# Processing the experts of a mixture layer in an order made on the chip from their numbers of blocks

## The chip, the cores and the metric

The kernel runs on one core of a Trainium2 chip. The metric is the device time of one execution in microseconds (us). Three runs of the kernel before took 956.48, 958.35 and 960.37 us, median 958.35. The profiled execution took 958.9 us; its span, from the first to the last instruction of the core, is 956.8 us.

## The reference

One encoder layer over 768 tokens of width 1024 (256 of a prompt, 512 of a sample): an input projection, neighbourhood attention, a convolution module, an output projection, and then a mixture of 32 experts. Only the mixture matters here:

```
g_sel = argmax(h @ w_group + b_group)                  # one group of 4
top_v, top_j = top_k(h @ w_expert[g_sel] + b_expert, 2)  # two of its 8 experts
counts = bincount(expert_idx, length=32)
hid = silu(x_b @ w_gate[e]) * (x_b @ w_up[e])
y   = hid @ w_down[e]                                  # per block of rows of one expert
```

Gate and up weights are 1024 x 512, the down weight is 512 x 1024, all float32, so an expert has three matrices of 2 MB. The order in which experts are worked through does not enter the result. The two results of a token are weighted by its gates and added to it, and a final RMS norm follows.

## The kernel before

The routing is made on the chip. Each token picks two experts, and the rows of an expert are packed into blocks of 64 (BLK). An expert has as many blocks as its rows need, and at least one. With the reference's inputs the counts of rows give 39 blocks: experts 5, 7, 21, 24 and 31 have two, expert 28 has three, and the other 26 have one. Blocks are numbered from 0 to 38 in the order of the experts 0 to 31.

VectorE (DVE) computes the routing in one chain (lines 1750 to 1801): from the logits to one-hot choices, a running count `before`, two matmuls on TensorE (PE) that give each token's rank within its expert (lines 1172 and 1173), the number of blocks of each expert (`nblk`), their running sum (`endb`, `startb`), from that the row that each token gets, and an index list `idx` (line 1801). DVE also writes `table`, integers in SBUF from which the engines read loop bounds: 32 numbers of blocks, 32 first blocks, 32 last blocks and two counts.

Weights lie in three slots. The experts at positions 0, 3, 6, ... use slot 0, those at 1, 4, 7, ... slot 1 (both in `ring`), those at 2, 5, 8, ... slot 2 (in `big`). Experts 0, 1 and 2 are loaded before the routing is known (lines 741 to 768). From then on SyncE (SP) runs `load_expert` (line 729) for positions 3 to 31: six transfers of 1 MB each, two halves of gate and up (the first pair when PE has passed the first half of the gate and up work of the last block that uses the slot, the second pair when it has passed the second), and two halves of down when the block's down work is done. All go through SP's one queue, in this order.

PE runs `expert` (line 1246) for the 32 positions: for each block, gate and up matmuls (lines 1201 and 1204), which wait for the four halves one by one, then transposes of the hidden rows and of the next block's rows (lines 1216 and 1192), then down matmuls (lines 1238 and 1239), which wait for the two down halves. ScalarE (ACT) applies Silu, DVE multiplies, and ACT and DVE take the result out of PSUM with the gates (line 1840 is DVE's part, the last work of a block but for the store). GpSimd (POOL) gathers the 64 rows of a block from DRAM four blocks ahead (line 885, 256 KB), and stores the results by an indirect transfer into `results` (line 900, 256 KB).

The last two blocks (37 and 38) are not stored. When the store of block 36 has landed, SP issues twelve reads of 512 KB of `results` into slot 2 (lines 778 to 782). POOL adds them in pairs (line 955), DVE adds the first four pairs to `x` (line 1851) right after the last block's result, PE adds the last two blocks by one-hot matmuls (line 1268; for tiles 4 and 5 also the pairs, line 1271), DVE takes each tile's sum (line 1890), ACT squares, POOL takes the root (line 830), DVE scales (line 1895) and SP stores the output (line 785).

## Time and profile before

| | us |
|---|---|
| median of three runs | 958.35 (956.48 to 960.37) |
| profiled execution | 958.9 |
| its span | 956.8 |
| PE busy | 851.9 (89% of the span) |
| DVE busy | 425.4 (44%) |
| ACT busy | 248.9 (26%) |
| POOL busy | 156.7 (16%) |

The page gives busy times of the engines over the whole span, then the span in 40 equal slices of 23.92 us with the DMA engines' busy share and what they moved, then the chain of work that ended last and the costliest groups of instructions. The expert stage begins at about 399 us and its last block ends at 925 us; what lies before is the same in both kernels but for a few constants. "Busy" of DMA is the mean over the core's 16 DMA engines.

### The profile page before, as it was taken

Reading aid. Unit: us, or ns where it says so; the run is one execution under the profiler, and the core shown is the slowest. Engines: PE = TensorE matmul, PEld = TensorE weight load, DVE = VectorE, ACT = ScalarE, POOL = GpSimd, SP = SyncE. Lnnn points to the kernel's source line nnn. Section 1 sums busy time; section 2 is a strip of 40 time slices with the busy share of each in tenths; the row PEclk is TensorE's granted clock in tenths of the full one; section 3 lists DMA queues with packets and bytes.
Section 4 is the critical chain, followed back from the end, with each engine's and each line's share of the span. In section 5 each row is a group of like instructions: output and inputs, shape, how many; then the busy total and the mean of one; then the engine's idle time right before and its main releaser. Section 6 shows DMA issues by size and latency. Waiting matters only on the chain.

```text
span 956.8 us, 15627 instructions
## 1 busy us (share of the span) xinstructions
PE 851.9 (89%) x5808; PEld 579.0 (61%) x5809; DVE 425.4 (44%) x622; ACT 248.9 (26%) x486; POOL 156.7 (16%) x286
## 2 busy tenths in 40 slices
PE   3989999999869995599999998888789989889985
PEld 2879978778558884455555554444445556455542
DVE  5399979857987433522222221212121222122265
ACT  5214273664655222011111111111011111111112
POOL 4100010000001000212222222111112222121162
PEclk9989999999979996599999999999999999999997
DMA  7443435221084637699999999999999999999464
GB/s 200 121 123 107 157 143 187 68 77 45 4 245 192 253 143 292 243 356 405 390 399 398 397 405 400 413 403 416 401 412 412 392 393 387 399 402 396 160 242 132
DMA packets 80891, 265.75 MB, mean 278 GB/s; under 512 B 18093, under 2 KB 43949, under 8 KB 56281
## 3 DMA queue, kind: packets, MB, share of 16 engines
q1 hardware_dynamic: 63232, 245.10, 67.2%
q0 software_dynamic: 7808, 18.54, 5.6%
q10 hardware_dynamic: 9816, 1.66, 0.9%
q8 instruction: 21, 0.34, 0.1%
q14 instruction: 14, 0.11, 0.0%
HBM read 247.52 MB, written 27.08 MB: 287 GB/s over the span
## 4 chain that ended last, share of the span: by engine, by line
PE 64%; DMA 17%; SPq 8%; DVE 6%; issue 2%; ACT 1%; ACTq 0%; POOL 0%; POOLq 0%; DVEq 0%
PE ps L1201 15%; PE ps L999 12%; DMA ring<-in_w_up 10%; PE ps L1238 9%; SPq L723 7%; PE ps L1121 7%; PE ps L995 4%; DMA ring<-in_w_down 3%; DMA big<-in_w_up 3%; PE ps L1204 3%; PE ps L1192 2%; DVE big L1585 2%; PE ps L1216 2%; PE ps L1018 1%; PE ps L1048 1%
## 5 line engine op out<-in xcount | busy, mean ns | idle before, releaser
L1204 PE MATMUL ps<-ring,big 128*64 128x256 f32 x896 | 208.5, 391 | 23.6 <-DMA ring<-in_w_up 23.5
L1201 PE MATMUL ps<-ring,big 128*64 128x256 f32 x896 | 210.2, 391 | 3.7 <-DMA ring<-in_w_gate 2.5
L1201 PEld LDWEIGHTS ps<-ring,big 128*64 128x64 f32 x896 | 124.3, 141 | 60.8 <-issue 15.4
L1204 PEld LDWEIGHTS ps<-ring,big 128*64 128x64 f32 x896 | 124.8, 141 | 54.0 <-DMA ring<-in_w_up 32.2
L1831 DVE TENSOR_TENSOR big<-ps,big 64x256 f32<-64x256 f32 x78 | 33.2, 426 | 263.9 <-ACT big L1482 263.9
L999 PE MATMUL ps<-hT,w_split 128*128 128x512 f32 (+1 forms) x768 | 145.2, 344 | 4.1 <-DVE hT L1541 3.6
L999 PEld LDWEIGHTS ps<-hT,w_split 128*128 128x128 f32 x768 | 118.0, 190 | 25.6 <-issue 11.3
L1585 DVE SCALAR_TENSOR_TENSOR big<-big,vec 128x783 f32<-128x783 f32 x116 | 119.6, 1031 | 3.0
L1482 ACT ACTIVATE big<-ps 64x256 f32<-64x256 f32 x78 | 29.3, 375 | 285.9 <-PE ps L1204 285.9
L1238 PE MATMUL ps<-ring,big 128*64 128x512 f32 x224 | 102.3, 599 | 0.3 <-DMA ring<-in_w_down 0.3
L1239 PE MATMUL ps<-ring,big 128*64 128x512 f32 x224 | 102.4, 599 | 0.0
L1204 PE MATMUL ps<-big 128*64 128x256 f32 x352 | 80.2, 386 | 7.1 <-DMA big<-in_w_up 7.1
L1840 DVE TENSOR_SCALAR big<-ps,gate_of 64x512 f32<-64x512 f32 x39 | 29.5, 756 | 122.5 <-PE ps L1239 122.5
L1201 PE MATMUL ps<-big 128*64 128x256 f32 x352 | 80.7, 385 | 0.5 <-DMA big<-in_w_gate 0.5
L897 POOL COPY to_of<-idx 64x1 uint32 x37 | 18.7, 506 | 331.4 <-DVE big L1840 331.4
L1121 PE MATMUL ps<-wo_split,hT 128*128 128x512 f32 x288 | 70.2, 402 | 2.1 <-issue 2.1
L1121 PEld LDWEIGHTS ps<-wo_split,hT 128*128 128x128 f32 x288 | 55.0, 194 | 13.4 <-issue 2.1
L1201 PEld LDWEIGHTS ps<-big 128*64 128x64 f32 x352 | 48.4, 139 | 23.6 <-issue 5.2
L1494 ACT ACTIVATE big<-ps,gate_of 64x512 f32<-64x512 f32 x39 | 26.6, 681 | 131.7 <-PE ps L1239 131.7
L1238 PEld LDWEIGHTS ps<-ring,big 128*64 128x64 f32 x224 | 28.1, 136 | 50.5 <-issue 48.7
L1204 PEld LDWEIGHTS ps<-big 128*64 128x64 f32 x352 | 48.4, 139 | 16.8 <-DMA big<-in_w_up 9.9
L1192 PE MATMUL ps<-ident,spare 64*128 64x64 f32 x320 | 41.9, 272 | 1.2 <-DVE spare L1856 1.2
(213 smaller groups left out, 1119.4 us busy)
## 6 DMA issues: line engine op xcount, KB each, us to landing
ring<-in_w_gate SPq DMA_DIRECT2D x44, 1024.0 KB, 28.0
ring<-in_w_up SPq DMA_DIRECT2D x44, 1024.0 KB, 28.8
ring<-in_w_down SPq DMA_DIRECT2D x44, 1024.0 KB, 29.4
big<-in_w_gate SPq DMA_DIRECT2D x20, 1024.0 KB, 29.0
big<-in_w_up SPq DMA_DIRECT2D x20, 1024.0 KB, 29.6
big<-in_w_down SPq DMA_DIRECT2D x20, 1024.0 KB, 29.2
w_raw<-in_w_in SPq DMA_DIRECT2D x20, 512.0 KB, 4.0
results<-spare POOLq DMA_DIRECT2D x12, 512.0 KB, 2.9
```

The lines of the kernel that those rows point to most:

```text
L723: sp.dma_start(to[:, ks, :], src).then_inc(landed, 16)
L995: mm = pe.matmul(ps[:, n % 2, 0:2 * P], hT[:, k // 4, hi_h, k % 4, g * P:(g + 1) * P], split_of(2 * c)[:, :, hi_w, k, :], **flags)
L999: mm = pe.matmul(ps[:, n % 2, 0:size], w_split[:, sub, hi_w, k, :], hT[:, k // 4, hi_h, k % 4, cols], **flags)
L1121: mm = pe.matmul(ps[:, OUT_BANK[g], :], mT[:, part, hi_m, k, t * P:(t + 1) * P], wo_split[n % 2][:, hi_w, k, :], start=(k == 0 and m == 0) ...
L1192: mm = pe.transpose(ps[:, 4, k * BLK:(k + 1) * BLK], xb[:, k:D:KD], ident[0:BLK, 0:BLK])
L1201: pe.matmul(ps[0:BLK, 6 * h, 0:FH], xT[:, k, :], gate_w[s][:, k, fs], start=(k == 0), stop=(k == KD - 1))
L1204: mm = pe.matmul(ps[BLK:2 * BLK, 6 * h + 1, 0:FH], xT[:, k, :], up_w[s][:, k, fs], start=(k == 0), stop=(k == KD - 1))
L1238: pe.matmul(ps[0:BLK, 2, :], hbT[:, k, :], down_w[s][:, k, 0:512], start=(k == 0), stop=(k == KF - 1))
L1239: mm = pe.matmul(ps[BLK:2 * BLK, 3, :], hbT[:, k, :], down_w[s][:, k, 512:1024], start=(k == 0), stop=(k == KF - 1))
L1585: link(nc.vector.scalar_tensor_tensor(conv[:, j % 2, :], z, w, conv[:, j % 2, :], ALU.mult, ALU.add))
L1831: nc.vector.tensor_tensor(hb[:, fs], ps[BLK:2 * BLK, 6 * h + 1, 0:FH], sG[:, fs], ALU.mult).then_inc(hb_ready[h], 1)
L1840: nc.vector.tensor_scalar(yb2[q][:, 512:1024], ps[BLK:2 * BLK, 3, :], gate_of[q][BLK:2 * BLK], None, ALU.mult).then_inc(evacuated, 1)
```

## The change

Experts 0, 1 and 2 stay first. The other 29 are ranked by their number of blocks, more first, the lower number first among equals, and a fixed pattern `PLACES` says which rank goes to which position (place): ranks 20 to 23 to places 3 to 6, ranks 24 to 28 (the fewest blocks) to places 27 to 31, ranks 6 down to 0 (the most blocks) to places 8, 11, 14, ..., 26, and the rest to the places between. Blocks are numbered by places. The order is made in the routing chain: DVE writes a key, compares all pairs of keys, PE sums the comparisons over partitions, DVE finds the place of each expert, PE and DVE turn the numbers of blocks into running sums by place and back to the experts' numbers, and `table` gets 32 entries more, the expert at each place. SP reads the expert from the table before it loads a place.

With the counts of the reference's inputs the places get the experts 0, 1, 2, 19, 20, 22, 23, 18, 3, 11, 17, 31, 10, 16, 24, 9, 15, 21, 8, 14, 7, 6, 13, 5, 4, 12, 28, 25, 26, 27, 29, 30. The numbers of blocks by place are 1 at places 0 to 10, then 2 1 1 2 1 1 2 1 1 2 1 1 2 1 1 3 at places 11 to 26, and 1 at places 27 to 31. By places before they are 1 1 1 1 1 2 1 2, then 1 at places 8 to 20, then 2 1 1 2 1 1 1 3 1 1 2.

```diff
+PLACES = [((0, 3, 1), E - 3, 1), ((8, 27, 3), 6, -1), ((9, 25, 3), 12, -1), ((7, 26, 3), 19, -1), ((3, 7, 1), 20, 1), ((27, 32, 1), 24, 1)]
+AT_ONCE = 3
 NB = MAXB + 2
...
@@ -727,9 +738,9 @@
                     load(e, *l)
             def load_expert(i, s):
-                e = SLOTS * i + s
-                end = sp.value_load(table[0:1, bass.ds(e + (2 * E - SLOTS), 1)], min_val=1, max_val=MAXB)
+                place = SLOTS * i + s
+                e = sp.value_load(table[0:1, bass.ds(place + (3 * E + 2), 1)], min_val=0, max_val=E - 1)
+                end = sp.value_load(table[0:1, bass.ds(place + (2 * E - SLOTS), 1)], min_val=1, max_val=MAXB)
                 sp.wait_ge(gu_half, end)
                 load_some(e, s, 0, 2)
...
             nc.gpsimd.memset(onesr[:], 1.0).then_inc(consts, 1)
+            link(nc.gpsimd.iota(key_first, [[-1, E]], base=0, channel_multiplier=0, allow_small_or_imprecise_dtypes=True))
+            nc.gpsimd.iota(key_first[:, 0:AT_ONCE], [[-BLK * MAXB, AT_ONCE]], base=-BLK * MAXB, channel_multiplier=0,
+                           allow_small_or_imprecise_dtypes=True).then_inc(consts, 1)
+            for (first, end, step), rank, by in PLACES:
+                nc.gpsimd.iota(rank_at[:, first:end:step], [[by, len(range(first, end, step))]], base=rank, channel_multiplier=0,
+                               allow_small_or_imprecise_dtypes=True).then_inc(consts, 1)
+            nc.gpsimd.memset(ends[:, 0:1], 0.0).then_inc(consts, 1)
             def root(out, in_, scale, ready, n):
...
@@ -1167,10 +1186,21 @@
-            pe.wait_ge(both_ready, 1)
+            pe.wait_ge(order_ready, 1)
             n = SLOTS8 * E - 1
             pe.matmul(ps[:, 0, 0:n], ones[:], before[:, 0:n], start=True, stop=False)
-            pe.matmul(ps[:, 0, 0:n], tri[:], both[:, 1:n + 1], start=False, stop=True).then_inc(rank_done, 1)
+            pe.matmul(ps[:, 0, 0:n], tri[:], both[:, 1:n + 1], start=False, stop=True).then_inc(order_ps, 1)
+            pe.wait_ge(x2_done, len(OUT))
+            pe.wait_ge(order_ready, 2)
+            pe.matmul(ps[0:E, 1, 0:1], behind, ones[0:E, 0:1], start=True, stop=True).then_inc(order_ps, 1)
+            pe.wait_ge(order_ready, 3)
+            pe.matmul(ps[:, 3, 0:E], column[:, 1:2].to_broadcast([E, P]), from_place, start=True, stop=True).then_inc(order_ps, 1)
+            pe.wait_ge(order_ready, 4)
+            pe.matmul(ps[:, 1, E:2 * E], column[:, 2:3].to_broadcast([E, P]), ident[0:E, 0:E], start=True, stop=True).then_inc(order_ps, 1)
+            pe.matmul(ps[:, 3, E:2 * E], token[0:E, 0:1].to_broadcast([E, P]), at_place, start=True, stop=True).then_inc(order_ps, 1)
             for a in range(2 * NT):
...
@@ -1759,17 +1789,36 @@
                 link(V.tensor_tensor(sel[:, j].rearrange("p t (g e) -> p t g e", g=G), within_groups(j), in_group, ALU.mult))
             dve.wait_ge(zero_out, 16 * ZERO_TILES)
             link(V.tensor_tensor(both.rearrange("p (e t) -> p t e", t=SLOTS8)[:, 1:NT + 1, :], sel[:, 0], sel[:, 1], ALU.add))
-            V.tensor_tensor_scan(before, again[:], both, 0.0, ALU.mult, ALU.add).then_inc(both_ready, 1)
+            V.tensor_tensor_scan(before, again[:], both, 0.0, ALU.mult, ALU.add).then_inc(order_ready, 1)
             V.tensor_tensor(dd[:], m2[:], m1[:], ALU.subtract).then_inc(dd_ready, 1)
-            dve.wait_ge(rank_done, 1)
+            dve.wait_ge(order_ps, 1)
             rank = ps[:, 0, 0:SLOTS8 * E].rearrange("p (e t) -> p e t", t=SLOTS8)
+            rank_sb = rank_in.rearrange("p (e t) -> p e t", t=SLOTS8)
+            own = ident[0:E, 0:E]
+            def own_column(n, row):
+                return V.tensor_tensor_reduce(out=row_of, in0=row, in1=own if n < 2 else at_place, scale=1.0, scalar=0.0,
+                                              op0=ALU.mult, op1=ALU.add, accum_out=column[:, n:n + 1])
             link(V.tensor_tensor(cmpb, rank[:, :, NT:NT + 1].to_broadcast([P, E, MAXN]),
                                  thr[:].unsqueeze(1).to_broadcast([P, E, MAXN]), ALU.is_gt))
             link(V.tensor_reduce(nblk[:], cmpb, AX.X, ALU.add))
-            link(V.tensor_tensor_scan(endb[:], onesr[:], nblk[:], 0.0, ALU.mult, ALU.add))
-            link(V.tensor_tensor(startb[:], endb[:], nblk[:], ALU.subtract))
-            link(V.scalar_tensor_tensor(pos, startb[:].unsqueeze(2).to_broadcast([P, E, NT]), float(BLK), rank[:, :, 0:NT],
+            link(V.scalar_tensor_tensor(key, nblk[:], float(BLK), key_first, ALU.mult, ALU.add))
+            link(own_column(0, key[0:E]))
+            V.tensor_scalar(behind, key[0:E], column[:, 0:1], None, ALU.is_lt).then_inc(order_ready, 1)
+            link(own_column(1, nblk[0:E]))
+            dve.wait_ge(order_ps, 2)
+            link(V.tensor_scalar(at_place, rank_at[0:E], ps[0:E, 1, 0:1], None, ALU.is_equal))
+            V.tensor_tensor_scan(from_place, onesr[0:E], at_place, 0.0, ALU.mult, ALU.add).then_inc(order_ready, 1)
+            link(V.tensor_copy(rank_in, ps[:, 0, 0:SLOTS8 * E]))
+            dve.wait_ge(order_ps, 3)
+            link(V.tensor_copy(ends[:, 1:], ps[:, 3, 0:E]))
+            own_column(2, ends[0:E, 0:E]).then_inc(order_ready, 1)
+            dve.wait_ge(order_ps, 4)
+            startb = ps[:, 1, E:2 * E]
+            link(V.scalar_tensor_tensor(pos, startb.unsqueeze(2).to_broadcast([P, E, NT]), float(BLK), rank_sb[:, :, 0:NT],
                                         ALU.mult, ALU.add))
             link(V.tensor_tensor(posd, sel, pos.rearrange("p e t -> p t e").unsqueeze(1).to_broadcast([P, 2, NT, E]), ALU.mult))
             link(V.tensor_reduce(destf[:], posd, AX.X, ALU.add))
@@ -1786,15 +1835,18 @@
                                      block_at[:, j].unsqueeze(2).to_broadcast([P, NT, NB]), ALU.is_equal))
                 V.tensor_tensor(block_hot[:, some], block_hot[:, some], token[:, some].unsqueeze(2).to_broadcast([P, NT, NB]),
                                 ALU.mult).then_inc(onehot_ready, 1)
-            link(V.tensor_copy(table[0:1, 0:E], nblk[0:1, :]))
-            link(V.tensor_copy(table[0:1, E:2 * E], startb[0:1, :]))
-            link(V.tensor_scalar(even[:], even[:], endb[0:1, E - 1:E], None, ALU.is_lt))
+            link(V.tensor_tensor(table[0:1, 0:E], ends[0:1, 1:], ends[0:1, 0:E], ALU.subtract))
+            link(V.tensor_copy(table[0:1, E:2 * E], ends[0:1, 0:E]))
+            dve.wait_ge(order_ps, 5)
+            link(V.tensor_scalar(table[0:1, 3 * E + 2:], ps[0:1, 3, E:2 * E], -1.0, None, ALU.add))
+            link(V.tensor_scalar(even[:], even[:], ends[0:1, E:], None, ALU.is_lt))
             link(V.tensor_reduce(cnt2[:, 0:1], even[:], AX.X, ALU.add))
-            link(V.scalar_tensor_tensor(cnt2[:, 1:2], cnt2[:, 0:1], -2.0, endb[0:1, E - 1:E], ALU.mult, ALU.add))
+            link(V.scalar_tensor_tensor(cnt2[:, 1:2], cnt2[:, 0:1], -2.0, ends[0:1, E:], ALU.mult, ALU.add))
             link(V.tensor_scalar(cnt2[:, 1:2], cnt2[:, 1:2], -5.0, None, ALU.add))
-            link(V.tensor_copy(table[0:1, 3 * E:], cnt2[:]))
-            V.tensor_copy(table[0:1, 2 * E:3 * E], endb[0:1, :]).then_inc(table_ready, 1)
+            link(V.tensor_copy(table[0:1, 3 * E:3 * E + 2], cnt2[:]))
+            V.tensor_copy(table[0:1, 2 * E:3 * E], ends[0:1, 1:]).then_inc(table_ready, 1)
             dve.wait_ge(idx_ps, 1)
             link(V.tensor_scalar(nobody[:], ps[0:BLK, 5, 0:NB], 0.0, float(4 * T), ALU.is_equal, ALU.mult))
```

## Rows read from the trace of the kernel before

**Rows 1.** The page, part 2: what DMA moved in 40 slices of the span.
```profile
GB/s 200 121 123 107 157 143 187 68 77 45 4 245 192 253 143 292 243 356 405 390 399 398 397 405 400 413 403 416 401 412 412 392 393 387 399 402 396 160 242 132
```

**Rows 2.** Busy time by stretch of the expert stage; the columns are named above.
```profile
core 0: us, PE busy (x) PEld busy (x) DVE busy (x) ACT busy (x) POOL busy (x), PEclk, DMA share, GB/s
399.00:545.00 146.00, 144.89 (x1100) 86.36 (x1101) 35.74 (x60) 23.14 (x59) 31.80 (x58) 0.97 0.96 374
...
580.00:732.00 152.00, 126.44 (x859) 68.78 (x859) 28.07 (x48) 18.57 (x49) 24.32 (x45) 0.97 1.02 407
732.00:865.00 133.00, 124.48 (x922) 74.20 (x920) 29.78 (x50) 19.77 (x50) 27.01 (x50) 0.99 1.02 395
865.00:901.00 36.00, 36.00 (x280) 21.31 (x278) 8.96 (x15) 5.95 (x15) 6.71 (x12) 1.00 0.80 312
...
```

**Rows 3.** DVE in order of time: the last work of blocks 20, 32, 36, 37, 38.
```profile
682.76 0.76 DVE L1840 TENSOR_SCALAR big<-ps,gate_of 64x512 f32<-64x512 f32 x1 [3.25 <-PE ps L1239]
...
853.26 0.75 DVE L1840 TENSOR_SCALAR big<-ps,gate_of 64x512 f32<-64x512 f32 x1 [3.80 <-PE ps L1239]
...
901.26 0.76 DVE L1840 TENSOR_SCALAR big<-ps,gate_of 64x512 f32<-64x512 f32 x1 [3.26 <-PE ps L1239]
...
913.25 0.76 DVE L1840 TENSOR_SCALAR big<-ps,gate_of 64x512 f32<-64x512 f32 x1 [3.26 <-PE ps L1239]
925.24 0.76 DVE L1840 TENSOR_SCALAR big<-ps,gate_of 64x512 f32<-64x512 f32 x1 [0.57 <-PE ps L1239]
```

**Rows 4.** Chain of waits in order of time: three weight loads (start of issue, us).
```profile
645.90 27.90 DMA ring<-in_w_up
...
739.85 34.61 DMA ring<-in_w_up
...
821.20 29.85 DMA ring<-in_w_down
```

**Rows 5.** SP's queue in order of time: the first issues for places 7 and 8.
```profile
455.84 0.34 SPq L723 DMA_DIRECT2D ring<-in_w_gate  x1
...
479.82 0.34 SPq L723 DMA_DIRECT2D big<-in_w_gate  x1
```

**Rows 6.** DMA from 880 to 920 us, in slices of 1 us.
```profile
GB/s 401 426 426 438 311 287 266 365 316 254 254 229 188 266 188 180 102 115 102 70 25 16 0 0 0 111 0 131 385 430 377 410 414 422 418 422 406 418 414 418
```

**Rows 7.** The routing and the first block, in order of time, several engines.
```profile
384.37 0.22 DVE L1770 TENSOR_TENSOR_SCAN endb<-onesr,nblk 128x32 f32<-128x32 f32 x1
384.62 0.19 DVE L1771 TENSOR_TENSOR startb<-endb,nblk 128x32 f32<-128x32 f32 x1
384.85 0.35 DVE L1772 SCALAR_TENSOR_TENSOR big<-startb,ps 128x192 f32<-128x192 f32 x1
...
397.92 0.71 DVE L1856 COPY spare<-big 64x1024 f32<-64x1024 f32 x1 [3.22 <-DMA big<-h_rows,idx_of]
...
398.77 1.11 PE L1192 MATMUL ps<-ident,spare 64*128 64x64 f32 x8 [1.20 <-DVE spare L1856]
399.92 0.69 DVE L1820 COPY big<-ps 128x512 f32<-128x512 f32 x1 [1.29 <-PE ps L1192]
```

**Rows 8.** POOL in order of time, the first operation after its constants.
```profile
7.31 0.19 POOL L830 TENSOR_SCALAR r<-ss 128x1 f32<-128x1 f32 x1 [3.62 <-ACT big L1297]
```

**Rows 9.** The tail: SP's issues, DVE and PE, in order of time.
```profile
906.20 5.82 SPq L782 DMA_DIRECT2D big<-results  x12
...
926.02 5.33 DVE L1851 TENSOR_TENSOR x<-x,big 128x1024 f32<-128x1024 f32 x4
931.39 2.35 DVE L1890 TENSOR_TENSOR x<-x,ps 128x1024 f32<-128x1024 f32 x2
...
932.66 6.25 PE L1268 MATMUL ps<-big 128*128 128x512 f32 x10 [2.85 <-DVE x L1890]
```

**Rows 10.** POOL's pair sums (line 955) and the landing of the reads (line 782).
```profile
L955 POOL TENSOR_TENSOR big<-big x6: 2354/2360/2865, 911.3 to 924.0; 128x1024 f32<-128x1024 f32 x6
...
DMA to landing us min/median/max: 3.7/8.1/12.3
```

More of the change, by code:

```diff
@@ L524, in encoder @@
         nblk = sb("nblk", [P, E])
-        onesr = sb("onesr", [P, E]); endb = sb("endb", [P, E]); startb = sb("startb", [P, E])
+        ends = sb("ends", [P, E + 1])
+        onesr = sb("onesr", [P, E]); column = sb("column", [E, 4]); rank_in = after(SLOTS8 * E)
+        key, behind, at_place, from_place, row_of = (
+            junk[0:n, 2 * NT * NB + k * E:2 * NT * NB + (k + 1) * E] for k, n in enumerate((P, E, E, E, E)))
         again = sb("again", [P, SLOTS8 * E]); silu_first = sb("silu_first", [P, 1])
@@ L545, in encoder @@
         row_gates = sb("row_gates", [P, NB])
+        key_first, rank_at = row_gates[:, 0:E], row_tokens[:, 0:E]
         gate_of = [sb(f"gate_of{q}", [P, 1]) for q in range(2)]
         even = sb("even", [1, MAXPAIRS]); cnt2 = sb("cnt2", [1, 2])
-        table = sb("table", [1, 3 * E + 2], I32)
+        table = sb("table", [1, 4 * E + 2], I32)
         ps = ctx.enter_context(nc.psum_tensor("ps", [P, 8, 512], F32))
@@ L772, in _ @@
                     load_expert(i, s)
-            for e in range(E // SLOTS * SLOTS, E):
-                load_expert(e // SLOTS, e % SLOTS)
+            for place in range(E // SLOTS * SLOTS, E):
+                load_expert(place // SLOTS, place % SLOTS)
             pairs = sp.value_load(table[0:1, 3 * E:3 * E + 1], min_val=(E - 7) // 2, max_val=MAXPAIRS)
@@ L963, in _ @@
         def _(pe):
-            pe.wait_ge(consts, 14)
+            pe.wait_ge(consts, CONSTS)
             def turn_h(t):
@@ L1245, in _, with expert @@
             turn_rows()
-            def expert(e, s, target):
-                n = pe.value_load(table[0:1, bass.ds(e, 1)], min_val=1, max_val=MAXN)
-                first = pe.value_load(table[0:1, bass.ds(e + E, 1)], min_val=0, max_val=MAXB - 1)
+            def expert(place, s, target):
+                n = pe.value_load(table[0:1, bass.ds(place, 1)], min_val=1, max_val=MAXN)
+                first = pe.value_load(table[0:1, bass.ds(place + E, 1)], min_val=0, max_val=MAXB - 1)
                 with pe.Fori(0, n) as j:
@@ L1254, in _ @@
                     expert(SLOTS * i + s, s, 16 * i + 16)
-            for e in range(E // SLOTS * SLOTS, E):
-                expert(e, e % SLOTS, 16 * (e // SLOTS + 1))
+            for place in range(E // SLOTS * SLOTS, E):
+                expert(place, place % SLOTS, 16 * (place // SLOTS + 1))
             pe.wait_ge(late_ready, 1)
```

11 lines of the change are left out of this document (6 added, 5 removed).

## The prediction

> **What bounds the kernel now.** I read the page's slices first, then the stretches of the expert stage, then the ends of single blocks, the landings in the chain of waits, SP's queue, and last the routing chain and the tail. The slices show DMA at 385 to 416 GB/s from about 430 to 885 us [rows 1]. That is the stream of weights: 29 experts after the first three, 6 MB each. The stretches show two regimes [rows 2]. From 399 to 545 us PE is busy all the time (144.9 of 146 us), since three experts were loaded ahead. From 580 on PE waits (126.4 busy of 152 us), and DMA's share is 1.02: the stream is the bound there. From 865 to 901 PE is full again and DMA is not, because the stream runs out before the work does.
>
> A block that waits for nothing takes 12.0 us (913.25 to 925.24) [rows 3]. The stream's pace is 16.8 us per place: the last up half of place 18 landed at 645.90 + 27.90 = 673.80 and that of place 24 at 739.85 + 34.61 = 774.46, 16.8 each for six places [rows 4]. The last down half of place 28 landed at 821.20 + 29.85 = 851.05 [rows 4] and the last weights of all at about 901.5, where the slices of 1 us fall to nothing [rows 6], again 16.8 each for three places. So experts of one block starve PE, those of two (24 us) feed it, and the seven surplus blocks are worth something only while the stream still runs.
>
> The end is the point. Expert 28 has three blocks (the first ended at 853.26 [rows 3]) and expert 31 two, so when the last weights landed PE had just ended block 36 (901.26) and still had 37 and 38 to do, till 925.24 [rows 3]. That is 24 us of PE work behind the end of the stream, and then the tail: 956.8 - 925.2 = 31.6 us.
>
> **The change part by part.**
>
> *Length of the stream.* 29 places of 6 MB before and after, one after another. The first load waits for block 0 as before. In the front the new order has one block per place up to place 10; SP issues the load of place p+3 when the last block of place p has passed its first half, so single blocks let it issue earlier: before, the double of expert 5 held the issue for place 8 back to 479.82, 24 us after that for place 7 [rows 5]. DMA's share from 399 to 545 us is 0.96, so some 6 of 146 us were idle, the start included [rows 2], and I take 1 to 2 us as gained. Against it, one more block's rows will have been stored by the end of the stream (256 KB, 0.7 us at 400 GB/s). After the triple the load of place 29 is issued some 15 us before the queue is empty: block three of place 26 passes its first half about 28 us after block one began, while the last weights of place 26 land about 9 us after that beginning and those of the places 27 and 28 take 33.6 us more, 43 in all. So no gap. I leave the end of the stream at 901.5, between 898 and 905.
>
> *Work behind the stream.* Place 31 now has one block. A block that waits for its weights ends (start of line 1840) 9.0 us after the last up half (673.80 to 682.76) and at least 2.2 us after the last down half (851.05 to 853.26) [rows 3, 4]. The two down halves take 2 x 16.8 / 6 = 5.6 us after the last up, so the end comes 9.0 - 5.6 = 3.4 us after the last landing: 904.9. The other bound is PE's own: the last up half of place 26, the triple, lands at 774.46 + 2 x 16.8 = 808.1, its first block ends at 817.1, and seven more blocks of 12.0 follow: 901.1. The later counts, 904.9; with the pace a little slower in the middle both would meet near 905. Does PE reach place 26 in time? A group "2 1 1" takes 48 us of PE and 50.3 of the stream, so it arrives a little early each time. Before the routing's cost this is 925.2 - 904.9 = 20.3 us earlier.
>
> *The routing chain.* It is on the path: nothing of the expert stage starts before it. Removed are the sum and the difference at lines 1770 and 1771, 384.37 to 384.85, 0.48 us [rows 7]. Added on DVE ahead of the rows' places: key, own column, comparison, place, running sum, copy, own column, seven operations on 32 columns or less, at 0.19 to 0.22 us from those two rows and 0.03 between, 1.6 us. The copy of the ranks (256 columns, near the 0.35 us of line 1772 [rows 7]) and the second own column lie in the shadow of PE. Added are three round trips from DVE to PE and back. The nearest row is the one of eight transposes: DVE ends at 398.63, PE takes 398.77 to 399.88, DVE starts at 399.92, 1.3 us [rows 7]. With one small matmul instead of eight I take 0.8 each, between the bare handoffs of that row (0.14 and 0.04, say 0.2) and 1.3: 2.4 us, bounds 0.6 to 3.9; it is nearer to the upper row, whose work is of the same kind. One more operation stands ahead of the index list, 0.2. The sum is 1.6 + 2.4 + 0.2 - 0.5 = 3.7, taken as 4, with bounds of 2 and 5.5. All of the expert stage shifts by it, its stream too. The nine new constants of POOL at the start are hidden by the 3.6 us that POOL then waits for the first square sum [rows 8]; that holds while each takes under 0.4 us, and if one took more only the excess would count. SP's extra table read per place costs nothing while its queue is ahead by 28 us [rows 4]. Last work of block 38: 904.9 + 4 = 908.9, the stream's end 905.5.
>
> *The tail.* Before, SP issued the twelve reads of `results` at 906.20, 19 us before the last block ended [rows 9], on idle DMA; they landed 3.7 to 12.3 us after issue [rows 10], all ahead of use. A store lands 5 us after its block's end (901.26 to 906.20) [rows 3, 9]. Now the store of block 36 (place 29, two places of 16.8 us before 908.9) lands at about 880, and the reads stand in SP's queue behind the last weights. Loads land in the order of their issue at a steady pace [rows 4], so I let the reads land behind 905.5, 1.28 us each at the 410 GB/s of the reads in [rows 6]. Pair 0 is there at 908.1, and POOL adds a pair in 2.36 us [rows 10], so pair 3 is done at 918.0 and DVE's fourth addition (1.33 us by 5.33 / 4 [rows 9]) at 919.3. Before, the first sum with the last blocks (line 1890) started at 931.39 [rows 9]; all behind it stays as it is, the PE stretch of 6.25 us included. 931.4 - 919.3 = 12.1 us earlier: of the 16.3 us by which the last block ends earlier, 4.2 go to the wait for the reads. If the reads came earlier nothing is lost: bounds 0 and 7.
>
> The rule that bears on it stands in the Trainium skill, "DMA: Bandwidth & Descriptors", section "Queues, rings and completion order": each DMA engine takes the descriptors of one ring in order, and goes round between rings of different queues. By it the reads do wait behind the weights, and the stores on POOL's queue don't; no row of before has a read behind a weight load. Without the rule the time would be that of rival 1.
>
> Sum: span 956.8 - 12.1 = 944.7. The profiled execution lies 2.1 us above its span (958.9), so 946.8, and 0.55 above the median of 958.35: **946** us.
>
> **The rivals.** (1) The reads are not late: the sixteen engines of DMA don't finish together (the last weights trickle in from 885 to 901 [rows 6]), and the reads could fill that. Then the tail keeps its length: 942 us. (2) The stream starves somewhere, most likely after the triple, where the margin is smallest: if PE comes late to place 26 by one single block, the load of place 29 is issued late, and up to 7 us of stream are lost: 953. (3) The order doesn't do what it says (ranks or ties come out otherwise, or a place has another number of blocks): then only the 4 us of routing remain, 962. (4) Slower than before: the clock. PE now waits for weights from place 7 on, 90 us earlier than before. From block 7 (401 us, when the rows of block 0 are ready [rows 7], 3 more for its start at the low clock, and 7 x 12.0: 488) to 909 there are 421 us for 32 blocks, 13.2 us for each, so the plan holds down to a mean clock of 12.0 / 13.2 = 0.91 of full speed, and from 0.88 on all of the gain is gone. At 0.85 a block takes 14.1 us, 32 of them 452, and the time is 977. Against it: in the stretch where PE waits most today the clock is 0.97 [rows 2], with the same kind of waits, 4.8 us per single place.
>
> By the Trainium skill, "TensorE: Matmul & The Clock Gate", section "HAM oscillation — how this bites in real kernels", a stream of matmuls that waits for DMA at every tile can fall to the low clock at every tile; that would make rival 4 the forecast, with 977. The trace disagrees so far, by the 0.97.
>
> **How the numbers follow.** The forecast has 0.70, rival 1 0.12, rival 2 0.09, rival 3 0.05, rival 4 0.04. The range takes in the end of the stream (-3.5, +3.5), the routing (-2, +1.5) and the reads (-4.2, +2.8), whose full sums are 946 - 9.7 and 946 + 7.8; cut a little below, where three ends would have to meet, and with rivals 1 and 2 inside: 937 to 955. A measurement of this kernel tells some 0.5% from no change, which is below 953.6. Faster: 0.70 + 0.12 + two thirds of 0.09 = 0.88. Same: 0.03 + 0.05 = 0.08. Slower: 0.04.
>
> **What would show it.** The last weights land about as far after the routing as before, and only one block ends behind them, 3 to 4 us later. PE operations of lines 1201's kind on `big` (slot 2) go from 11 blocks to 17. PE starts to wait near place 7, about 490 us, and waits in small pieces to the end; its clock stays above 0.95. The first gate and up matmuls start about 4 us later. POOL's pair sums wait for reads, and DVE's four additions wait for POOL. I am wrong if the stream has a gap of more than 5 us, if the clock falls below 0.9, or if the routing takes over 7 us more.

## The result and the profile after

The changed kernel took 952.12 us in the median of four runs (950.59 to 953.14), the kernel before 958.95 on the same occasion (956.48 to 960.37). The ratio is 0.993, 95% interval 0.9905 to 0.9955: faster by 0.7%, or 6.8 us. The forecast was 946 (937 to 955), about 12 us faster. The sign, the range and the main mechanism held, but little more than half of the forecast gain came. The profiled execution has a span of 950.2 us against 956.8.

The end of the stages shows where it went. Below are two views of the changed kernel: what DMA moved by slice (the page, part 2), and busy time by stretch, columns as in [rows 2].

```profile
GB/s 202 120 120 117 155 143 188 68 79 45 1 222 221 211 188 240 280 263 405 403 390 399 404 415 399 396 399 393 402 401 396 401 404 390 406 383 405 394 208 133
```

```profile
core 0: us, PE busy (x) PEld busy (x) DVE busy (x) ACT busy (x) POOL busy (x), PEclk, DMA share, GB/s
403.00:545.00 142.00, 132.74 (x988) 78.45 (x990) 31.56 (x53) 20.27 (x51) 29.39 (x55) 0.97 0.96 377
545.00:580.00 35.00, 32.52 (x220) 17.95 (x218) 7.21 (x13) 4.91 (x13) 5.42 (x10) 0.95 1.01 402
580.00:732.00 152.00, 145.22 (x1102) 87.01 (x1098) 35.84 (x60) 23.87 (x60) 32.55 (x60) 1.00 1.02 399
732.00:865.00 133.00, 127.71 (x970) 75.41 (x968) 31.31 (x52) 20.57 (x51) 27.39 (x51) 1.00 1.01 398
865.00:906.00 41.00, 40.76 (x316) 24.42 (x312) 10.29 (x20) 7.00 (x18) 5.85 (x12) 1.00 0.99 395
906.00:924.00 18.00, 7.28 (x25) 2.45 (x24) 12.55 (x6) 0.96 (x2) 15.32 (x6) 0.79 0.49 199
```

The stream fills one slice more than before [rows 1], and DMA is at 0.99 up to 906 us, where before it had fallen to 0.80 in the last 36 us of the stream [rows 2]. PE's waits moved to the front (132.7 busy of 142 us), and in the stretch where it waited most before it is now nearly full (145.2 of 152, against 126.4), since the surplus blocks lie there. The clock is 0.95 or more in every stretch up to 906 us, so rival 4 is out.

DVE's last work of the blocks 37 and 38, to be compared with [rows 3]:

```profile
896.90 0.76 DVE L1892 TENSOR_SCALAR big<-ps,gate_of 64x512 f32<-64x512 f32 x1 [3.26 <-PE ps L1269]
909.76 0.76 DVE L1892 TENSOR_SCALAR big<-ps,gate_of 64x512 f32<-64x512 f32 x1 [2.79 <-PE ps L1269]
```

Block 38 reaches this point at 909.76, where 908.9 was forecast and 925.24 was the time before: 15.5 us earlier. But the span ends only 6.6 us earlier. The tail from this point to the end of the span was 956.8 - 925.2 = 31.6 us and is 950.2 - 909.8 = 40.4. It grew by 8.9 us, and 4.2 were forecast. Here is the tail in order of time, DVE and then POOL and SP; [rows 9] and [rows 10] answer to it.

```profile
910.93 1.22 DVE L1903 TENSOR_TENSOR x<-x,big 128x1024 f32<-128x1024 f32 x1 [0.41 <-POOL big L974]
914.39 9.91 DVE L1903 TENSOR_TENSOR x<-x,big 128x1024 f32<-128x1024 f32 x3 [2.23 <-POOL big L974]
924.33 2.35 DVE L1942 TENSOR_TENSOR x<-x,ps 128x1024 f32<-128x1024 f32 x2
...
908.55 17.96 POOL L974 TENSOR_TENSOR big<-big 128x1024 f32<-128x1024 f32 x6 [13.81 <-DMA big<-results]
...
893.99 13.35 SPq L793 DMA_DIRECT2D big<-results  x12
```

SP issued the reads at 893.99, and POOL could add the first pair at 908.55, as forecast (908.1). From there on it is slower than forecast. DVE's additions 2 to 4 take 9.91 us together, 3.3 each, where they took 5.33 / 4 = 1.33 before, and POOL's six pair sums fill 17.96 us without a gap, 3.0 each. DVE's fourth addition ends at 924.3, not at 919.3.

The groups of the two lines show the same by minimum, median and maximum in ns:

```profile
L974 POOL TENSOR_TENSOR big<-big x6: 2330/3316/3337, 908.5 to 923.2; 128x1024 f32<-128x1024 f32 x6
...
L1903 DVE TENSOR_TENSOR x<-x,big x4: 1224/3352/3356, 910.9 to 920.9; 128x1024 f32<-128x1024 f32 x4
...
L1942 DVE TENSOR_TENSOR x<-x,ps x6: 1211/1220/1221, 924.3 to 938.4; 128x1024 f32<-128x1024 f32 x6
```

Beside a pair sum of POOL, an addition of DVE that reads two tiles of SBUF takes 3.35 us instead of 1.22, and POOL's takes 3.32 instead of 2.33. The sums of line 1942, of the same size but with one operand in PSUM, take 1.22 throughout, the first of them beside POOL's last pair sum.

### The profile page after: what moved, and what is told of

It reads as the page before. It is cut to its first block, busy times and chain, and to the rows that moved or that the text cites. A ratio compares the mean times of both kernels' runs of the same rounds, so it can differ in the third digit from the quotient of the medians.

```text
span 950.2 us, 15799 instructions
## 1 busy us (share of the span) xinstructions
PE 845.7 (89%) x5816; PEld 579.1 (61%) x5817; DVE 428.7 (45%) x633; ACT 249.2 (26%) x486; POOL 161.5 (17%) x295
## 4 chain that ended last, share of the span: by engine, by line
PE 56%; DMA 23%; SPq 8%; DVE 7%; issue 2%; ACT 1%; POOL 1%; ACTq 0%; POOLq 0%; DVEq 0%
DMA big<-in_w_up 17%; PE ps L1018 12%; PE ps L1231 10%; PE ps L1140 7%; SPq L734 7%; PE ps L1268 7%; PE ps L1014 4%; DMA ring<-in_w_down 3%; PE ps L1234 2%; DVE big L1615 2%; PE ps L1222 2%; DMA big<-results 2%; PE ps L1037 1%; PE ps L1067 1%; PE ps L1246 1%
## 5 line engine op out<-in xcount | busy, mean ns | idle before, releaser
L1234 PE MATMUL ps<-ring,big 128*64 128x256 f32 x704 | 159.3, 384 | 6.7 <-DMA ring<-in_w_up 6.7
L1231 PE MATMUL ps<-ring,big 128*64 128x256 f32 x704 | 159.6, 384 | 1.7 <-DVE big L1872 1.1
L1018 PE MATMUL ps<-hT,w_split 128*128 128x512 f32 (+1 forms) x768 | 145.2, 344 | 4.0 <-DVE hT L1571 3.5
L1234 PE MATMUL ps<-big 128*64 128x256 f32 x544 | 123.7, 384 | 15.1 <-DMA big<-in_w_up 15.1
L1018 PEld LDWEIGHTS ps<-hT,w_split 128*128 128x128 f32 x768 | 117.9, 190 | 25.5 <-issue 11.2
L1231 PEld LDWEIGHTS ps<-ring,big 128*64 128x64 f32 x704 | 97.1, 139 | 58.0 <-issue 14.9
L1231 PE MATMUL ps<-big 128*64 128x256 f32 x544 | 124.4, 384 | 0.5 <-DMA big<-in_w_gate 0.5
L1234 PEld LDWEIGHTS ps<-ring,big 128*64 128x64 f32 x704 | 97.3, 139 | 14.0 <-DMA ring<-in_w_up 8.9
L1234 PEld LDWEIGHTS ps<-big 128*64 128x64 f32 x544 | 74.1, 138 | 33.7 <-DMA big<-in_w_up 20.5
L1231 PEld LDWEIGHTS ps<-big 128*64 128x64 f32 x544 | 74.2, 138 | 30.5 <-issue 8.1
L1268 PE MATMUL ps<-ring,big 128*64 128x512 f32 x176 | 80.4, 599 | 0.2 <-DMA ring<-in_w_down 0.2
L1269 PE MATMUL ps<-ring,big 128*64 128x512 f32 x176 | 80.4, 599 | 0.0
L1269 PE MATMUL ps<-big 128*64 128x512 f32 x136 | 62.4, 600 | 0.0
L1268 PE MATMUL ps<-big 128*64 128x512 f32 x136 | 62.3, 599 | 0.0
```

The source lines that it names most:

```text
L1018: mm = pe.matmul(ps[:, n % 2, 0:size], w_split[:, sub, hi_w, k, :], hT[:, k // 4, hi_h, k % 4, cols], **flags)
L1231: pe.matmul(ps[0:BLK, 6 * h, 0:FH], xT[:, k, :], gate_w[s][:, k, fs], start=(k == 0), stop=(k == KD - 1))
L1234: mm = pe.matmul(ps[BLK:2 * BLK, 6 * h + 1, 0:FH], xT[:, k, :], up_w[s][:, k, fs], start=(k == 0), stop=(k == KD - 1))
L1268: pe.matmul(ps[0:BLK, 2, :], hbT[:, k, :], down_w[s][:, k, 0:512], start=(k == 0), stop=(k == KF - 1))
L1269: mm = pe.matmul(ps[BLK:2 * BLK, 3, :], hbT[:, k, :], down_w[s][:, k, 512:1024], start=(k == 0), stop=(k == KF - 1))
```

## The experiments

The theory after the result: (a) the order puts the end of PE's work some 20 us earlier, less 4 us for the routing, by way of the stream of weights and what stands behind it; (b) the tail grew because the reads land late and because POOL's and DVE's sums, which lay under PE's last blocks before, now run at the same time and hinder each other. The rivals were that only the end of the order matters, that something else in the change made or cost the time, and for the tail that the late reads alone are the cause, or none of both. All kernels but one are edits of the changed kernel; times are medians beside runs of the kernel before on the same chip (958.2 to 958.6).

**The chain without the order.** Keys and places give back the experts' numbers.

```diff
-PLACES = [((0, 3, 1), E - 3, 1), ...]
+PLACES = [((0, 32, 1), 0, 1)]
...
-            link(nc.gpsimd.iota(key_first, [[-1, E]], base=0, ...))
+            link(nc.gpsimd.iota(key_first, [[-BLK * MAXB, E]], base=0, ...))
```

> The changed kernel with its whole ordering chain, but with keys and places that give back the order of the experts' numbers. If the new order is worth what the traces suggest and the routing chain costs the 4.25 us by which the first expert matmul moved (401.00 to 405.25), this takes the time of before plus 4.2 us, near 963 us, with blocks 37 and 38 behind the end of the stream again. If part of the gain came from something else in the change (index and rows read from SBUF instead of PSUM, SP's loop), it is nearer to before, or below.

963.33 us, ratio 1.0056 (1.0038 to 1.0074), 4.8 us above before. The stretches before and after the last weights have again the numbers of before (DMA was at 0.80 in the last 36 us of the stream [rows 2]):

```profile
865.00:905.00 40.00, 40.00 (x300) 23.23 (x301) 9.91 (x17) 6.33 (x17) 6.72 (x12) 1.00 0.82 320
905.00:929.00 24.00, 24.00 (x188) 14.04 (x182) 8.91 (x13) 3.97 (x10) 14.51 (x12) 1.00 0.68 267
```

So the chain costs 4 to 5 us (3.6 to 7.1 by the interval), and the order alone brings 963.3 - 952.1 = 11.2 us. The first expert matmul moved by 4.25 us, so nothing else in the change is worth more than the noise.

**Most blocks first.** The places from 3 on in falling order.

```diff
-PLACES = [((0, 3, 1), E - 3, 1), ...]
+PLACES = [((0, 3, 1), E - 3, 1), ((3, 32, 1), 0, 1)]
```

> The changed kernel with the experts of most blocks at places 3 to 8 (triple first) and single blocks from 9 on. Theory (a slot is reloaded only when its expert's last block is half done, so multiple blocks in the front hold SP's issues back and leave DMA idle): the stream ends some 36 us later, block 38 ends near 945 to 950 us and the time is near 985 us. Rival (only the end of the order matters, since DMA's work is the same): within 3 us of the changed kernel, 952.

987.19 us, ratio 1.0307 (1.0272 to 1.0342). In the stretch of the triple and the doubles DMA is at 0.82, where the changed kernel and the one with the order of numbers have 0.96:

```profile
405.00:545.00 140.00, 139.40 (x1070) 82.78 (x1072) 34.11 (x58) 22.22 (x56) 31.22 (x58) 0.99 0.82 303
545.00:732.00 187.00, 177.04 (x1327) 102.30 (x1324) 43.08 (x73) 28.73 (x73) 37.82 (x70) 1.00 0.96 372
```

PE is full there and the stream is not; what the stream lost it never makes good, and single blocks at the end don't help. The last down matmul of block 38 ends at 944.4, 35 us later than in the changed kernel. The rival that only the end matters falls.

**Fewest first.** The places from 3 on in rising order, the triple last.

```diff
+PLACES = [((0, 3, 1), E - 3, 1), ((3, 32, 1), 28, -1)]
```

> The changed kernel with the places from 3 on in rising order of blocks: all single blocks first, the doubles at places 26 to 30, the triple at 31. Theory: the stream never starves, so its last weights land as in the changed kernel or some us earlier, but about 50 us of PE work stand behind it: block 38 ends near 956 us, the reads are early and the tail is 32 us, the time is near 990 us.

996.46 us, ratio 1.0398 (1.0366 to 1.0430), 6 us more than expected. The mechanism is the expected one: from 905 us on PE is full and DMA idle, until the reads come.

```profile
801.00:905.00 104.00, 99.97 (x766) 58.99 (x768) 25.35 (x42) 16.59 (x41) 22.71 (x42) 1.00 0.92 357
905.00:944.00 39.00, 39.00 (x308) 23.28 (x306) 9.29 (x16) 6.34 (x16) 7.47 (x15) 1.00 0.12 27
```

Its block 38 ends at 962.0 instead of 956. The first expert matmul was 1.2 us later than in the changed kernel, and PE reached the first double only at 801 us; the rest of the 6 us I didn't resolve.

**The surplus side by side.** Single blocks at both ends, the triple and the doubles at places 11 to 16.

```diff
+PLACES = [((0, 3, 1), E - 3, 1), ((11, 17, 1), 0, 1), ((3, 11, 1), 6, 1), ((17, 32, 1), 14, 1)]
```

> The changed kernel with single blocks at both ends as before (places 3 to 10 and 17 to 31), but the triple and the five doubles side by side at places 11 to 16. Theory (what counts besides the end is that a double at every third place lets SP issue early enough): DMA runs dry in the cluster, the stream ends some 12 to 14 us later, block 38 ends near 923 us, the time is near 965 us. Rival (fewest at both ends is all that matters): 952.

969.22 us, ratio 1.0117 (1.0089 to 1.0145), 17 us above the changed kernel. The stream runs thin behind the cluster:

```profile
580.00:640.00 60.00, 60.00 (x462) 35.46 (x460) 14.94 (x25) 9.96 (x25) 13.56 (x25) 1.00 0.97 373
640.00:732.00 92.00, 92.00 (x710) 54.16 (x708) 22.36 (x37) 14.90 (x37) 21.61 (x40) 1.00 0.85 315
```

15% of 92 us are 14 us, most of the loss. "Fewest at both ends" is thus only half of the change; a surplus block at every third place is the other half.

**The triple early.** Triple at place 8, doubles at 11 to 23, a single at 26.

```diff
-... ((8, 27, 3), 6, -1), ...
+... ((8, 27, 3), 0, 1), ...
```

> The changed kernel with the experts of most blocks in the other direction: the triple at place 8, doubles at 11 to 23, a single at 26. Theory: the last eight blocks of the changed kernel run on PE without a wait since the triple, and end just when the last weights allow it, so both bounds meet. With the triple early only the weights bound the end: block 38 ends within 1.5 us of the changed kernel and the time is 951 to 953 us. If PE had been the bound there by more, it is faster by that; if the triple at place 8 starves the stream, slower.

951.33 us, ratio 0.9932 (0.9908 to 0.9955): the same. From the first expert matmul to the last down matmul it is 504.35 us here and 504.36 in the changed kernel, although here PE waits for weights in each of the last places (34.4 busy of 40 us) and there in hardly any (40.8 of 41). So in the changed kernel the bound by the stream and the bound by PE meet, as the prediction worked out.

**A double at the last place.**

```diff
-... ((8, 27, 3), 6, -1), ... ((27, 32, 1), 24, 1)]
+... ((8, 9, 1), 6, -1), ((11, 12, 1), 28, 1), ((14, 27, 3), 4, -1), ... ((27, 31, 1), 24, 1), ((31, 32, 1), 5, 1)]
```

> The changed kernel with one expert of two blocks moved from place 11 to place 31, for a single one. PE then has 12 us more behind the last weights, so block 38 ends near 921 us. Theory (the tail of the changed kernel is 9 us longer than before because the reads of the results land behind the weights and the sums then collide): the 12 us cover the reads, the tail is again 31 to 33 us, and the time is only 2 to 4 us above the changed kernel, near 955. Rival (the tail is longer for a reason that has nothing to do with the reads): 12 us above, 964.

957.25 us, ratio 0.9992 (0.9977 to 1.0007). Block 38's last down matmul ends at 921.14, 11.5 us later than in the changed kernel, but the time is only 5.1 us higher, nearer to the theory than to its rival, with the tail 954.8 - 921.1 = 33.7 us. The 1 to 2 us over the expected tail are again a collision. These are DVE's rows while POOL's pair sums run, and two of POOL's; the operation of 128 x 768 took 0.96 us in the changed kernel, where POOL was idle at that time:

```profile
919.55 3.13 DVE L1932 TENSOR_TENSOR big<-lane,late_at 128x768 f32<-128x768 f32 x1
922.71 0.76 DVE L1893 TENSOR_SCALAR big<-ps,gate_of 64x512 f32<-64x512 f32 x1
923.50 5.87 DVE L1904 TENSOR_TENSOR x<-x,big 128x1024 f32<-128x1024 f32 x4
...
919.51 2.35 POOL L975 TENSOR_TENSOR big<-big 128x1024 f32<-128x1024 f32 x1 [0.21 <-DMA big<-results]
922.02 2.86 POOL L975 TENSOR_TENSOR big<-big 128x1024 f32<-128x1024 f32 x1 [0.15 <-DMA big<-results]
```

The two take turns. POOL's sum that began first kept its 2.35 us, and DVE's operation ended at 922.68, 0.8 us after that sum (921.86). POOL's next sum began while DVE was still at it and took 0.5 us more.

**DVE adds both halves.** POOL keeps the pair sums of tiles 4 and 5.

```diff
-            for t in range(NT):
+            for t in range(BY_VECTOR, NT):
                 pool.wait_ge(taken_in[t], 32)
...
-                dve.wait_ge(pair_done, t + 1)
-                nc.vector.tensor_tensor(x[:, t, :], x[:, t, :], taken_at[t][:, 0, :], ALU.add).then_inc(pair_added, 1)
+                dve.wait_ge(taken_in[t], 32)
+                link(nc.vector.tensor_tensor(x[:, t, :], x[:, t, :], taken_at[t][:, 0, :], ALU.add))
+                nc.vector.tensor_tensor(x[:, t, :], x[:, t, :], taken_at[t][:, 1, :], ALU.add).then_inc(pair_added, 1)
```

> The changed kernel with the four pair sums of tiles 0 to 3 taken from POOL: DVE adds both halves of a pair to x itself, POOL adds the pairs of tiles 4 and 5 alone. Theory (POOL's and DVE's additions of 1024 columns slow each other: 3.35 us each for DVE in place of 1.21, 3.32 for POOL in place of 2.36): DVE's eight additions take 1.2 us each, all over by 920.5 in place of 924.3, and the time falls by some 4 us to 948. Rival (the reads' landing alone sets the pace, one pair each 2.5 us): no change, 952, or up to 3 us more for the longer work of DVE.

949.71 us, ratio 0.9918 (0.9892 to 0.9943), 2.4 us below the changed kernel, where some 4 were expected; the intervals of the two overlap. From DVE's last work of block 38 to the end of the span it is 946.4 - 908.5 = 37.9 us here and was 40.4. Twice as many additions are over sooner, since seven of eight take 1.22 us. Reads were still landing beside them (DMA moved 104 GB/s from 911 to 922 us), so the landing itself does not slow an addition. The eighth meets POOL's pair sum of tile 4 and takes 3.25:

```profile
916.46 1.22 DVE L1903 TENSOR_TENSOR x<-x,big 128x1024 f32<-128x1024 f32 x1
917.71 3.25 DVE L1904 TENSOR_TENSOR x<-x,big 128x1024 f32<-128x1024 f32 x1
...
917.24 5.93 POOL L974 TENSOR_TENSOR big<-big 128x1024 f32<-128x1024 f32 x2 [23.66 <-DMA big<-results]
```

**The same edit in the kernel before.**

> The kernel before with the same change of the tail that brought the changed kernel from 952.1 to 949.7: DVE adds both halves for tiles 0 to 3. Theory: before, POOL's pair sums lay under PE's last 24 us, so they cost nothing, and four more additions of 1.2 us on DVE stand on the path: 5 us slower, 963. If DVE's additions are cheaper than POOL's anywhere, it is faster here too.

963.34 us, ratio 1.0058 (1.0035 to 1.0080), 4.8 us slower. What helps in the changed kernel hurts in the one before, where POOL's sums lay under PE's work. The edit isn't better by itself; its cover has gone.

**One half added.** As in the kernel with DVE's additions of both halves, but DVE adds one half only, so the result lacks the other half of tiles 0 to 3; the diff is against that kernel.

```diff
-                link(nc.vector.tensor_tensor(x[:, t, :], x[:, t, :], taken_at[t][:, 0, :], ALU.add))
-                nc.vector.tensor_tensor(x[:, t, :], x[:, t, :], taken_at[t][:, 1, :], ALU.add).then_inc(pair_added, 1)
+                nc.vector.tensor_tensor(x[:, t, :], x[:, t, :], taken_at[t][:, 0, :], ALU.add).then_inc(pair_added, 1)
```

> The changed kernel; POOL adds only the pairs of tiles 4 and 5, DVE adds only the first half of the results of tiles 0 to 3 (the second half is read but left out of the sum). This leaves the lateness of the reads and takes the collision away. Theory: the fourth addition ends 1.2 us after its read has landed, at 917, in place of 924.3, and the time is 945 us, 7 below the changed kernel. If the reads' landing were the whole cause it would be at most 2.4 us (POOL's own pair sum) below, 950.

944.22 us, ratio 0.9853 (0.9832 to 0.9873), 7.9 us below the changed kernel. With 942.6 - 909.8 = 32.8 us the tail is nearly as short as before. DVE's additions follow the reads:

```profile
910.62 2.36 DVE L1903 TENSOR_TENSOR x<-x,big 128x1024 f32<-128x1024 f32 x2
913.47 1.23 DVE L1903 TENSOR_TENSOR x<-x,big 128x1024 f32<-128x1024 f32 x1 [0.48 <-DMA big<-results]
915.97 1.23 DVE L1903 TENSOR_TENSOR x<-x,big 128x1024 f32<-128x1024 f32 x1 [1.27 <-DMA big<-results]
```

**One half read.** And the other half of tiles 0 to 3 isn't read.

```diff
-                for j in range(2):
+                for j in range(1 if t < BY_VECTOR else 2):
                     sp.dma_start(taken_at[t][:, j, :], ...).then_inc(taken_in[t], 16)
...
-                dve.wait_ge(taken_in[t], 32)
+                dve.wait_ge(taken_in[t], 16)
```

> As the kernel with one half added, but the second half of the results of tiles 0 to 3 is not read either (8 reads in place of 12). This takes the lateness away too. Theory: the four additions follow the last block's result at once, as in the kernel before, the tail from the last block's end to the end of the span is 31 to 32 us as there, and the time is 943 us; the difference to the kernel with one half added, 2 to 3 us, is what the reads behind the weights cost. If the late reads had cost all of the 9 us by which the tail grew, this run would be 9 us below the changed kernel and the other one near 950.

944.57 us, ratio 0.9858 (0.9838 to 0.9878): no gain over the one before, where 2 to 3 us were expected. The reads are in time now (no wait for DMA below), but with them POOL's sum of tile 4 starts earlier and meets DVE's fourth addition:

```profile
909.46 6.78 DVE L1903 TENSOR_TENSOR x<-x,big 128x1024 f32<-128x1024 f32 x4
...
912.31 6.15 POOL L974 TENSOR_TENSOR big<-big 128x1024 f32<-128x1024 f32 x2 [18.79 <-DMA big<-results]
```

Three of the additions end at 912.95, and the fourth takes 6.78 - 3.5 = 3.3 us of the group: the collision gives back the 2 us that the reads had cost.

**A busy PE.** DVE's additions of both halves for tiles 0 to 3, and more matmuls while PE waits; their result is not used.

```diff
+                if t == 2:
+                    for _ in range(8):
+                        pe.matmul(ps[:, 4, :], late_hot[:, 0, :], y_both[:, 0:512], start=True, stop=True)
```

> The kernel with DVE's additions for tiles 0 to 3, and eight more matmuls of 512 columns into an unused bank on PE between the second and the third tile, while PE waits for DVE. Theory (PE stands idle from 913 to 922 us and its next ten matmuls then take 6.7 us, at the low clock): they run at the high clock, the third and fourth tiles come 2 to 3 us earlier, and the time is 947 us, against 949.7 without. If DVE alone sets the pace there, nothing changes.

947.19 us, ratio 0.9890 (0.9865 to 0.9915), 2.5 us below the kernel without them; the two intervals overlap (0.9892 to 0.9943 there), but the profile shows a piece of 1.7 us. The first row is of the changed kernel (its mean clock was 0.65 from 913 to 924 us), the second of the kernel with DVE's additions alone (0.64 from 913 to 922), the third of this one (1.00 from 913 to 921):

```profile
925.60 6.74 PE L1298 MATMUL ps<-big 128*128 128x512 f32 x10 [11.27 <-DVE x L1942]
```

```profile
922.26 6.27 PE L1298 MATMUL ps<-big 128*128 128x512 f32 x10 [9.21 <-DVE x L1943]
```

```profile
923.56 4.56 PE L1301 MATMUL ps<-big 128*128 128x512 f32 x10 [2.35 <-DVE x L1946]
```

By the profiles the tail is 946.0 - 909.8 = 36.2 us against 37.9, and 6.27 - 4.56 is all of that.

**POOL after DVE.** The last kernel, and POOL waits with its two sums.

```diff
+            pool.wait_ge(pair_added, BY_VECTOR)
             for t in range(BY_VECTOR, NT):
                 pool.wait_ge(taken_in[t], 32)
```

> The kernel with DVE's additions and a busy PE (947.2 us), and POOL waits with its two pair sums until DVE's eighth addition is over. In the profile without this wait the eighth addition took 3.26 us beside POOL's sum, against 1.22 for the seven before it. Theory (two operations that both read two tiles of SBUF hinder each other, one that reads PSUM does not): the eighth takes 1.22 us, DVE's later sums with PSUM stay at 1.22 beside POOL, PE gets its pairs in time, and the time falls by 2 us to 945. If POOL's sums are then late for tiles 4 and 5, it stays at 947 or rises.

944.18 us, ratio 0.9850 (0.9830 to 0.9869): the fastest kernel that computes everything, 8 us below the changed one and 3 below the last, where 2 were expected. DVE's eighth addition takes 1.23 us, POOL's pair sums take 2.35 each, and they do not hinder the PSUM sums that run beside them:

```profile
918.11 1.23 DVE L1908 TENSOR_TENSOR x<-x,big 128x1024 f32<-128x1024 f32 x1
919.37 2.35 DVE L1947 TENSOR_TENSOR x<-x,ps 128x1024 f32<-128x1024 f32 x2
...
919.48 4.70 POOL L975 TENSOR_TENSOR big<-big 128x1024 f32<-128x1024 f32 x2 [25.86 <-DVE x L1908]
```

## Why the prediction was right, and where a term was mis-sized

*What bounds the kernel.* Right. The stream of weights has the same length under both orders as long as it isn't starved, and the gain is the PE work behind it: 24 us before, one block now. The order of numbers, with everything else of the change, lost it again.

*Length of the stream.* Right, "no gap" included: DMA's share is 1.01 or more from 545 to 865 us, and slot 2 had 17 blocks. The two starved orders show how near the other case lies.

*Work behind the stream.* Right: forecast 908.9, measured 909.76. That both bounds meet was confirmed by the triple at place 8.

*The routing chain.* Right in size, 4 forecast, 4.25 by the first expert matmul (the last row), 4.8 by the run with the order of numbers. Its parts, as rows of the changed kernel, to be read against [rows 7]:

```profile
384.96 0.18 DVE L1802 CUSTOM_DVE_ANT_0 big<-big,ident 32x32 f32<-32x32 f32 x1
385.18 0.23 DVE L1810 TENSOR_SCALAR big<-big,column 32x32 f32<-32x32 f32 x1
385.56 0.23 PE L1198 MATMUL ps<-ones,big 32*32 32x1 f32 x2 [2.04 <-DVE big L1810]
385.90 0.23 DVE L1813 TENSOR_SCALAR big<-row_tokens,ps 32x32 f32<-32x32 f32 x1 [0.38 <-PE ps L1198]
386.16 0.21 DVE L1814 TENSOR_TENSOR_SCAN big<-onesr,big 32x32 f32<-32x32 f32 x1
...
386.43 0.63 PE L1200 MATMUL ps<-big,column 32*128 32x32 f32 x2 [0.64 <-DVE big L1814]
387.17 0.19 DVE L1817 COPY ends<-ps 128x32 f32<-128x32 f32 x1 [0.48 <-PE ps L1200]
...
388.31 0.36 DVE L1821 SCALAR_TENSOR_TENSOR big<-ps,big 128x192 f32<-128x192 f32 x1 [0.72 <-PE ps L1202]
...
405.25 0.68 PE L1231 MATMUL ps<-ring,big 128*64 128x256 f32 x1 [1.11 <-DVE big L1872]
```

A round trip with one column took 0.49 us (385.41 to 385.90), those with 32 columns 0.8 and 0.7; 0.8 each was taken. The chain itself grew by some 3.1 us, forecast 3.7: the operation that gives the rows' places began at 388.31 against 384.85 [rows 7], and 0.36 of these 3.46 us lay ahead of the chain. The first matmul moved by more than that; 0.8 us of it is a longer wait for block 0's rows (4.05 us, 3.22 in [rows 7]). First matmuls lay between 403.7 and 406.5 us in the profiles of the other edits, so a part of the 4.25 is scatter.

*The tail.* This is the term that was mis-sized: 4.2 us forecast, 8.9 measured, which is outside the term's own bounds of 0 and 7. The total stayed in the range because the other terms came as forecast. The idea was right (what lay under PE's last blocks comes to light), and so was the landing of the first reads. But the prediction took durations of POOL (2.36) and DVE (1.33) from rows in which they hardly met, and let them run side by side at those. Counted from DVE's last work of block 38 to the first sum of the kind of line 1890, it was 6.2 us before and is 14.6 now; with POOL out of the way, but the reads as late as ever, it was 7.4 (909.8 to 917.23). So about 1 us of the growth comes from the landing of the reads as such, and 7 from having POOL's pair sums on the path: 0.4 + 2.2 us of waits for POOL and 3 x 2.1 us of slower additions, less 1.8 us of waits for reads that they cover. The reads' part and POOL's can't be told apart to better than 1 or 2 us, since the run without late reads met a collision again. The last 0.5 us of the 8.9 lie behind that sum: PE's ten matmuls took 6.74 us against 6.25 [rows 9].

The trace of before had the sign of it: in [rows 10] POOL's line 955 has a maximum of 2865 ns over a median of 2360. I read it as scatter. It is the sum that began while DVE's line 1879 was running, and on DVE the sign was plainer. Rows of the kernel before, DVE and then POOL:

```profile
914.04 2.67 DVE L1825 COPY spare<-big 64x1024 f32<-64x1024 f32 x1
...
921.54 3.12 DVE L1879 TENSOR_TENSOR big<-lane,late_at 128x768 f32<-128x768 f32 x1
...
911.32 4.84 POOL L955 TENSOR_TENSOR big<-big 128x1024 f32<-128x1024 f32 x2 [4.37 <-DMA big<-results]
...
921.49 2.36 POOL L955 TENSOR_TENSOR big<-big 128x1024 f32<-128x1024 f32 x1 [0.20 <-DMA big<-results]
924.00 2.87 POOL L955 TENSOR_TENSOR big<-big 128x1024 f32<-128x1024 f32 x1 [0.15 <-DMA big<-results]
```

The operation of 128 x 768 takes 0.96 us with POOL idle, the copy 0.69 (the median of its 39). The first of the four additions took 1.93 us and the others 1.21, so the 1.33 of the forecast was itself a mean over one that waited.

The Trainium skill has the collision as a rule, "GPSIMD Engine Reference", section "1. Specifications": GpSimd's interfaces to SBUF are shared with VectorE, and they contend with VectorE's instructions that have two SBUF inputs. The trace agrees: 3.35 against 1.22 us with two SBUF inputs, 1.22 beside POOL with one.

*The reads behind the weights.* Issued from 893.99 on, they landed 5.9 to 17.2 us after their issue, against 3.7 to 12.3 before [rows 10], and at the forecast times: the first pair could be added at 908.55 (908.1), and with one half added DVE could take tiles 2 and 3 at 913.47 and 915.97 (913.2 and 915.7 by the forecast's pace of 1.28 us a read). But the twelve reads are 6.3 MB, and from 906 to 924 us DMA moved only 3.6 MB (199 GB/s), so some 2.7 MB of them had moved earlier. So the reads did fill what the end of the stream leaves idle, as rival 1 had it, without landing earlier; that a read lands only with its slowest part is my reading, not shown engine by engine. By the Trainium skill, "DMA: Bandwidth & Descriptors", section "Queues, rings and completion order", each DMA engine takes the descriptors of one ring in order; these numbers agree with it. The store of block 36 took 6.7 us from issue to landing beside the stream, and SP could issue the reads 9.1 us after the block's end at 884.92, 5 before. I take it that this cost nothing, since the reads stood behind the weights; no run tests it.

*The rivals.* Reads not late (1): the tail would have had 31.6 us; it didn't. Starving after the triple (2): not here, but for other orders. Inert order (3) and clock (4): no. The clock was 0.95 or more in the stretches where PE waited for weights; the longest single wait for weights was 1.8 us. What the Trainium skill says in "TensorE: Matmul & The Clock Gate", section "HAM oscillation — how this bites in real kernels", of waits for DMA at every tile, by which it would have been 977, did not come about with waits of this kind.

## What to carry to other kernels

When a stream of loads is the bound, the order of the work is worth what it takes off the far side of the stream's end, and only if each surplus lies where the buffers still let the stream be issued ahead: a double at every third place was free, the triple and the five doubles side by side cost 17 us. Work taken off the end uncovers what lay under it, so size the tail anew, with durations from rows in which its engines run at once. Before giving POOL a share of elementwise work, look whether DVE will read two SBUF tiles, or copy from SBUF to SBUF, at that time; order one after the other, or let DVE do it. Look in the trace for one line with two clusters of duration.

## What the runs showed of the hardware that I had not expected

- An addition of 128 x 1024 float32 on DVE with both inputs in SBUF takes 1.22 us alone and 3.25 to 3.36 us beside an addition on POOL of the same size, which goes from 2.35 to 3.3. Side by side a pair of them takes 3.3 us, one after the other 1.22 + 2.35 = 3.6: the rows fit engines that take turns, the one that began later waiting for the other. The overlap gains next to nothing, and the shorter one pays for it. With one input in PSUM DVE keeps 1.22 us.
- It is not only operations with two inputs in SBUF. A copy of 64 x 1024 float32 on DVE from SBUF to SBUF took 2.67 us beside POOL's pair sums in the kernel before; in the same kernel with DVE's additions, where POOL was idle at that time, it took 0.69. Even an addition of 128 x 1 with both inputs in SBUF took 2.16 us in the kernel with the double last, and ended when POOL's sum did (919.31 and 919.30).
- Eight matmuls that compute nothing (16 instructions in the trace, 7.03 us), issued while PE waits for DVE, made the ten instructions after them take 4.56 us instead of 6.27.
